# Hybrid RWKV-7 / attention step: projections fed with x times coefficient, final norm by rows, x updated from PSUM

## What is computed

```python
def rmsnorm(x, g):
    return x * rsqrt(mean(x * x, -1) + RMS_EPS) * g
def modulate(h, shift, scale):
    return h * (1 + scale) + shift
...
for l in range(2):
    if l == 1:                                   # shared_kv
        h = modulate(rmsnorm(x, kv_norm_g), shift, scale)
        k, v = split(h @ w_kv + b_kv);  k = rope_partial(k, pos)
    h = modulate(rmsnorm(x, norm_g[l, 0]), sh1, sc1)
    y = time_mix(h) if l == 0 else window_attn(h @ at_w_q + at_b_q, k, v) @ at_w_o + at_b_o
    x = x + g1 * y
    h = modulate(rmsnorm(x, norm_g[l, 1]), sh2, sc2)
    x = x + g2 * hier_moe(h)                     # top 2 of 32 experts, silu(gate) * up, down
return rmsnorm(x, final_norm_g)
```

## Time and profile before

| | before |
|---|---|
| runs (us) | 1261.39, 1262.22, 1257.76; median 1261.39 |
| profiled execution: time, span | 1259.24, 1257.0 |
| busy: PE, DVE, ACT, POOL | 1103.0, 577.8, 339.5, 32.0 |
| mean granted clock of PE | 0.938 of full |
| bytes moved, mean rate | 304.95 MB, 243 GB/s |

### The profile page before, as it was taken

One profiled execution on the slowest core, in us unless ns is written; L12 is line 12 of the kernel. 1 busy time (PEld: TensorE's weight loads), 2 busy tenths in 40 slices (PEclk: granted clock), 3 DMA queues, 4 the chain that ended last, 5 costly groups with the idle time before them and its releaser, 6 DMA issues.

```text
span 1257.0 us, 23844 instructions
## 1 busy us (share of the span) xinstructions
PE 1103.0 (88%) x9637; PEld 646.9 (51%) x9637; DVE 577.8 (46%) x1446; ACT 339.5 (27%) x651; POOL 32.0 (3%) x50
## 2 busy tenths in 40 slices
PE   6699999999988884999999977987886799999983
PEld 3355555787887453344444435666654344444442
DVE  3802165654522536355555454243146355555554
ACT  1231140122213013333333222235213333333222
POOL 0200000000000002000000000000002000000000
PEclk9799999999999797999999998987897899999996
DMA  9868755665232553899999990052053599999951
GB/s 338 191 234 299 270 212 190 203 222 200 98 137 55 192 201 126 292 394 394 394 394 394 394 391 33 13 183 86 1 198 128 222 394 394 394 394 394 394 218 43
DMA packets 114934, 304.95 MB, mean 243 GB/s; under 512 B 7268, under 2 KB 8904, under 8 KB 107688
## 3 DMA queue, kind: packets, MB, share of 16 engines
q1 hardware_dynamic: 110544, 289.78, 62.5%
q0 software_dynamic: 4112, 13.97, 4.0%
q10 hardware_dynamic: 200, 0.06, 0.0%
HBM read 298.93 MB, written 4.86 MB: 242 GB/s over the span
## 4 chain that ended last, share of the span: by engine, by line
PE 59%; SPq 21%; DVE 8%; DMA 5%; issue 3%; ACT 3%; POOL 1%; ACTq 0%; DVEq 0%; POOLq 0%
PE bank L719 57%; SPq L533 15%; SPq L538 5%; DVE work L1538 2%; DMA ring<-in_moe_w_gu 2%; DMA ring<-in_ada_w 2%; ACT work L1289 2%; DVE work L1544 1%; DVE work L1541 1%; DMA work<-h_rows,work 1%; DVE rstd L1576 1%; POOL work L659 1%; DVE att L1985 1%; ACT ring L1289 0%; PE bank L1245 0%
## 5 line engine op out<-in xcount | busy, mean ns | idle before, releaser
L719 PE MATMUL bank<-ring,work 128*64 128x512 f32 (+1 forms) x1760 | 353.2, 553 | 24.8 <-DMA ring<-in_moe_w_gu 11.7
L719 PE MATMUL bank<-work,ring 128*128 128x320 f32 (+4 forms) x1648 | 305.1, 366 | 17.4 <-DVE work L1541 7.0
L719 PEld LDWEIGHTS bank<-work,ring 128*128 128x128 f32 (+3 forms) x1648 | 211.4, 168 | 121.5 <-issue 39.8
L719 PEld LDWEIGHTS bank<-ring,work 128*64 128x64 f32 (+1 forms) x1760 | 119.0, 138 | 234.4 <-issue 230.6
L719 PE MATMUL bank<-work 128*128 128x320 bf16 (+11 forms) x1732 | 198.9, 281 | 22.5 <-DVE work L1538 7.8
L719 PEld LDWEIGHTS bank<-work 128*128 128x128 bf16 (+2 forms) x1732 | 148.1, 122 | 89.4 <-issue 26.0
L1289 ACT ACTIVATE work<-bank 128x512 f32<-128x512 f32 (+5 forms) x111 | 53.8, 517 | 209.9 <-PE bank L719 155.1
L1901 DVE TENSOR_TENSOR work<-work,bank 128x320 f32<-128x320 f32 x256 | 107.4, 481 | 1.3 <-PE bank L719 1.3
L719 PEld LDWEIGHTS bank<-ring 64*64 64x64 f32 (+2 forms) x2624 | 89.3, 136 | 20.3 <-issue 12.6
L719 PE MATMUL bank<-ring 64*64 64x64 f32 (+2 forms) x2624 | 96.5, 225 | 3.1 <-issue 2.1
L1889 DVE TENSOR_REDUCE small<-bank 64x1 f32<-64x3 f32 x64 | 10.1, 158 | 166.6 <-PE bank L719 165.6
(11 more groups left out here) (190 smaller groups left out, 794.0 us busy)
## 6 DMA issues: line engine op xcount, KB each, us to landing
ring<-in_moe_w_gu SPq DMA_DIRECT2D x128, 1024.0 KB, 14.9
ring<-in_moe_w_down SPq DMA_DIRECT2D x64, 1024.0 KB, 13.9
ring<-in_ada_w SPq DMA_DIRECT2D x35, 1024.0 KB, 5.1
ring<-in_rw_w_rkv SPq DMA_DIRECT2D x6, 2048.0 KB, 7.8
ring<-in_ada_w SPq DMA_DIRECT2D x4, 2048.0 KB, 17.9
ring<-in_kv_ada_w SPq DMA_DIRECT2D x8, 1024.0 KB, 4.8
work<-in_ada_w SPq DMA_DIRECT2D x5, 1024.0 KB, 6.2
ring<-in_rw_w_o SPq DMA_DIRECT2D x2, 2048.0 KB, 11.7
```

Of the source, the lines that this page charges most:

```text
L719: return eng.matmul(out, l, r, start=start, stop=stop, **kw)
```

## The change

- **Projections fed early.** `hkv` and `haq` become x times `coef` (norm gain times 1 + scale), without the norm factor and without the shift. ACT makes `hkv` a chunk at a time as soon as that chunk of x is final, then `haq`. The shifts are two further columns (one for each sequence): 322 columns instead of 320. PE projects outputs 0 and 1 of `kv`, then does the sum of squares, then outputs 2 and 3. The squares are DVE's.
- **Factor at eviction.** DVE multiplies each output by the factor and adds the bias to the two shift columns (`scaled`); ACT adds those as the bias, for each sequence (`biased`). So an output is evicted by 4 instructions on 2 engines in place of 1.
- **x from PSUM.** In pair 15 DVE first adds the finished `ysum` to x (`sum_to_x`), then adds the results of pairs 14 and 15 straight from PSUM to x, two instructions a chunk. Pair 0's result is copied to `ysum`, so its memset goes. `y_added` starts at 8, not 1, with all waits on it moved to match.
- **Final norm by rows.** PE transposes x itself (chunks 0 to 3 once they are final, then 4 to 7); ACT squares the token rows from PSUM and sums along them; 3 short DVE operations and a root; 6 DVE products write `ytok`, and SP writes it out in 6 DMAs of half rows. `gain_row` is loaded by POOL, 128 copies of 4 KB.
- **Filler.** PE does 5 matmuls of 512 columns ahead of the gather's transposes and 4 behind them, into a bank that nobody reads.
- In layer 0 both `coefficients` move from behind the expert loop to just ahead of `passes`.

```diff
-hkv, haq, q, qt, oT = E[1], E[5], E[6], E[7], E[5]
+gain_row = wk(D)
+row_sq = wk(6).rearrange("p (j h) -> p j h", j=3)
+row_ms = wk(3)
+TS = T + 2
+q, qt, oT = E[6], E[7], E[5]
+haq = work[:, 6 * B - C * TS:6 * B].rearrange("p (c t) -> p c t", c=C)
+hkv = work[:, 8192 - C * TS:8192].rearrange("p (c t) -> p c t", c=C)
...
+    for j, (t0, k) in enumerate(TILES):
+        for hf in range(2):
+            cols = slice(512 * hf, 512 * hf + 512)
+            sp.wait("ytok", j, hf)
+            dst = o[1][0][:, cols] if j == 2 else o[0][0, t0:t0 + k, cols]
+            eng.dma_start(dst, ytok[0:k, j, cols]).then_inc(in_sems["y_written"], 16)
...
+    eng.dma_start(gain_row, i["final_norm_g"].rearrange("(a d) -> a d", a=1).broadcast_to([P, D])
+                  ).then_inc(in_sems["gain_in"], 16)
...
+    def keep_busy(n):
+        pb = bank.spare()
+        for _ in range(n):
+            ins = mm(pb[:, :], ident, const[:, 0:512], True, True)
+        pe.did(ins)
...
+        keep_busy(5)
...
+        keep_busy(4)
         pe.wait("passes", l)
...
-        pe.wait("x begun", l)
+        while bank.n % 8:
+            bank.n += 1
+        return nb
     moe(0)
+    project("kv", range(2), hkv, lambda hf: ("wkv",), ("h", "KV"))
     mean_square("A1")
-    project("kv", range(4), hkv, lambda hf: ("wkv",), ("h", "KV"))
+    pe.wait("x moe", 0)
+    project("kv", range(2, 4), hkv, lambda hf: ("wkv",))
...
+    pe.wait("shifts")
...
-    moe(1)
-    mean_square("F")
-    pe.wait("h", "F")
-    for j, (t0, k) in enumerate(TILES):
-        for hf in range(2):
-            pb = bank.open("ytok", j, hf)
+    nb = moe(1)
+    for hf in range(2):
+        eng.wait_ge(moe_sems[1]["y_added"], 128 * nb + 4 * hf + 4)
+        for j, (t0, k) in enumerate(TILES):
+            b = 3 * hf + j
+            if b == 3:
+                pe.wait("x moe", 1)
+            pb = bank.open("xt", j, hf)
             for cc in range(4):
-                ins = eng.transpose(pb[0:k, P * cc:P * cc + P], E[1][:, 4 * hf + cc, t0:t0 + k], ident)
-            full(ins, "ytok", j, hf)
+                ins = eng.transpose(pb[0:k, P * cc:P * cc + P], x[:, 4 * hf + cc, t0:t0 + k], ident)
+            full(ins, "xt", j, hf)
...
+    nb = moe(0)
+    ac.wait("coef", "A1")
+    for c in range(C):
+        eng.wait_ge(moe_sems[0]["y_added"], 128 * nb + c + 1)
+        for r, t0, k in SEQS:
+            act(hkv[:, c, t0:t0 + k], x[:, c, t0:t0 + k], ACT.Identity, ("h", "KV", c),
+                scale=coef2[:, 0, r, c:c + 1])
+    ac.wait("x moe", 0)
+    for c in range(C):
+        for r, t0, k in SEQS:
+            act(haq[:, c, t0:t0 + k], x[:, c, t0:t0 + k], ACT.Identity, ("h", "A1", c),
+                scale=coef2[:, 1, r, c:c + 1])
     root("A1")
-    modulated("KV", E[0], hkv)
...
+    def biased(n, dst, *keys):
+        ac.wait("scaled", n)
+        for r, t0, k in SEQS:
+            act(dst[:, t0:t0 + k], dst[:, t0:t0 + k], ACT.Identity, *keys, bias=bcol[:, n, r:r + 1])
+    for c in range(2):
+        biased(c, kraw[:, c, :], ("kraw", c))
+    for c in range(2):
+        biased(2 + c, vT[:, c, :], ("vT", c))
...
-        act(q[:, c, :], pk("q", c)[:, 0:T], ACT.Identity, ("read", "q", c), ("qraw", c),
-            bias=vcol("at_b_q", c))
+        biased(4 + c, q[:, c, :], ("qraw", c))
...
-    squares("F")
-    root("F")
...
+    act(small[0:1, 14:15], cst("ident")[0:1, 0:1], ACT.Sqrt)
+    ac.wait("sums zeroed", 1)
+    for hf in range(2):
+        for j, (t0, k) in enumerate(TILES):
+            act(work[0:k, 512 * (3 * hf + j):512 * (3 * hf + j) + 512],
+                pk("xt", j, hf)[0:k, :], ACT.Square, ("row squares", j, hf),
+                accum_out=row_sq[0:k, j, hf:hf + 1])
+    ac.wait("row ms")
+    act(row_ms, row_ms, ACT.Sqrt, ("row root",))
...
-        op(eng.memset(ysum[:, :, :], 0.0))
+        op(eng.memset(row_sq, 0.0), ("sums zeroed", l))
...
         op(eng.memset(xcols[:, :, NA:XC], 0.0))
+        if l == 0:
+            ve.wait("h", "B0", C - 1)
+            coefficients("KV", vcol("kv_norm_g", 0, C))
+            coefficients("A1", vcol("norm_g", 16, C))
...
-        def added(i, u, cc):
+        def gate(r, c):
+            return mod[:, l, r, 40 + c:40 + c + 1]
+        def added(i, u, cc, where):
             for c in cc:
                 eng.wait_ge(S["y_made"], 8 * i + c + 1)
-                eng.tensor_tensor(ysum[:, c, :], ysum[:, c, :], ps[y_bank(u, c)][:, 0:T],
-                                  A_).then_inc(S["y_added"], 1)
-        def pair(i, u, e_next, first_pair):
+                y = ps[y_bank(u, c)]
+                if where == "new":
+                    ins = eng.tensor_copy(ysum[:, c, :], y[:, 0:T])
+                elif where == "sum":
+                    ins = eng.tensor_tensor(ysum[:, c, :], ysum[:, c, :], y[:, 0:T], A_)
+                else:
+                    for r, t0, k in SEQS:
+                        ins = eng.scalar_tensor_tensor(x[:, c, t0:t0 + k], y[:, t0:t0 + k], gate(r, c),
+                                                       x[:, c, t0:t0 + k], M, A_)
+                ins.then_inc(S["y_added"], 1)
+        sums = 2 if l == 0 else 1
+        def sum_to_x(p):
+            for c in range(C):
+                for r, t0, k in SEQS:
+                    ins = eng.scalar_tensor_tensor(x[:, c, t0:t0 + k], ysum[:, c, t0:t0 + k], gate(r, c),
+                                                   x[:, c, t0:t0 + k], M, A_)
+            ins.then_inc(S["x_summed"], 1)
+            if l == 0:
+                eng.wait_ge(S["x_summed"], sums * p + 1)
+                for r in range(2):
+                    ins = eng.tensor_copy(hkv[:, :, T + r], kvmod[:, r, 0:C])
+                ins.then_inc(S["x_summed"], 1)
+        def pair(i, u, e_next, where, last=None):
+            if last is not None:
+                eng.wait_ge(S["y_added"], 8 * i)
+                sum_to_x(last)
+                eng.wait_ge(S["x_summed"], sums * last + sums)
             weigh(i, u)
-            if not first_pair:
-                added(i - 1, 1 - u, range(6))
+            if where:
+                added(i - 1, 1 - u, range(6), where)
...
-            if not first_pair:
-                added(i - 1, 1 - u, range(6, C))
+            if where:
+                added(i - 1, 1 - u, range(6, C), where)
             if e_next is not None:
...
-            pair(16 * p, 0, 4, True)
-            pair(16 * p + 1, 1, 4, False)
+            pair(16 * p, 0, 4, None)
+            pair(16 * p + 1, 1, 4, "new")
             with eng.Fori(1, EXP // 4 - 1) as k_:
                 for u in range(2):
-                    pair(16 * p + 2 * k_ + u, u, 4 * k_ + 4, False)
-            for u in range(2):
-                pair(16 * p + 14 + u, u, None, False)
-            added(16 * p + 15, 1, range(C))
+                    pair(16 * p + 2 * k_ + u, u, 4 * k_ + 4, "sum")
+            pair(16 * p + 14, 0, None, "sum")
+            pair(16 * p + 15, 1, None, "x", last=p)
+            added(16 * p + 15, 1, range(C), "x")
...
-        eng.wait_ge(S["y_added"], 128 * nb + 1)
-        for c in range(C):
-            for r, t0, k in SEQS:
-                stt(x[:, c, t0:t0 + k], ysum[:, c, t0:t0 + k], mod[:, l, r, 40 + c:40 + c + 1],
-                    x[:, c, t0:t0 + k], M, A_, *([("x begun", l)] if c == r == 0 else []),
-                    ("x for", "A1" if l == 0 else "F", c // 2))
+        eng.wait_ge(S["y_added"], 128 * nb + 8)
+        op(eng.memset(small[:, 13:14], 0.0), ("x moe", l))
         ve.settle()
     moe(0)
-    coefficients("KV", vcol("kv_norm_g", 0, C))
-    coefficients("A1", vcol("norm_g", 16, C))
+    for b in range(4):
+        tt_(sq_buf("A1")[:, 2 * b:2 * b + 2, :], x[:, 2 * b:2 * b + 2, :], x[:, 2 * b:2 * b + 2, :], M,
+            ("squares", "A1", b))
+    for r in range(2):
+        op(eng.tensor_copy(haq[:, :, T + r], mod[:, 1, r, 0:C]), ("shifts",))
     rms("A1")
     ve.settle()
-    normed("KV", E[0])
-    modulated("KV", E[0], hkv, range(C - ACT_CHUNKS))
-    modulated("A1", E[0], haq, range(C))
+    def scaled(n, dst, bias, *key):
+        pb = pk(*key)
+        ts(bcol[:, n, :], pb[:, T:TS], bias, None, A_, ALU.bypass)
+        tt_(dst, pb[:, 0:T], rstd[:, :], M, ("read",) + key, ("scaled", n))
+    for c in range(4):
+        scaled(c, kraw[:, c, :] if c < 2 else vT[:, c - 2, :], vcol("b_kv", c), "kv", c)
...
+    def rotated(c):
...
+    for c in range(C):
+        scaled(4 + c, q[:, c, :], vcol("at_b_q", c), "q", c)
+        if c:
+            rotated(c - 1)
+    rotated(C - 1)
...
-    rms("F")
+    eng.wait_ge(in_sems["gain_in"], 16)
+    for j in range(3):
+        ve.wait("row squares", j, 1)
+    op(eng.tensor_reduce(row_ms, row_sq, AX.X, A_))
     ve.settle()
-    normed("F", E[0])
-    for c in range(C):
-        ts(E[1][:, c, :], E[0][:, c, :], vcol("final_norm_g", c), None, M, ALU.bypass, ("h", "F"))
+    ts(row_ms, row_ms, 1.0 / D, RMS_EPS, M, A_, ("row ms",))
+    ve.wait("row root")
```

(7 more changed lines are left out.)

66 lines of the change are left out of this document (32 added, 34 removed).

## The result

| | before | after |
|---|---|---|
| runs beside each other (us) | 1256.63 to 1262.22, median 1259.58 | 1224.87 to 1233.28, median 1228.09 |
| profiled execution: time, span | 1259.24, 1257.0 | 1225.86, 1224.1 |
| mean granted clock of PE | 0.938 | 0.954 |

A forecast was written before the change was run, and what follows sets the result against it. Expert loops stream weights at the DMA's rate, the rest being short serial work. Terms +0.2 - 2.0 - 12.7 + 0.8 - 11.7 = -25.4 us gave 1233.8 to 1236.0, so 1235.0; range 1228 to 1243.

The forecast's parts named there:

- part 5: End of the kernel, from x whole through transposes, squares and products to the output writes: -11.7 us, bounds -9.5 and -13.
- 7.4 us of landing and closing to the span's end: Time from the last output DMA issue to the span's end in the old kernel; only 0.4 us less to land forecast.
- Part 1: Entry of the expert loops, with coefficients moved ahead and filler for PE's clock: +0.2 us in layer 0, -2.0 in layer 1.
- 0.9 of 1.8 in layer 0: Entry of layer 0's expert loop: filler gives back 0.9 of the 1.8 us lost at 1.2 GHz.
- Part 2: Last pair of each expert loop: sum_to_x hidden with 0.7 us to spare, adds ahead of the hidT copy cost PE +1.15 us.
- rival B: Last pair of each loop: sum_to_x isn't hidden, up to 5 us a layer; 1241 us for 3 a layer; 6%.
- Part 3: From layer 0's final scatter to the end of the KV projection: -12.7 us, bounds -10.5 and -14.
- over 0.27: Length in us of a 322-column matmul record above which such matmuls would count as slowed.
- rival D: Projections: 96 matmuls of 322 columns run slower than those of 320; 1288 us at twice as long; 3%.
- Rival C: KV projection, layer 0: ACT can start hkv only when x is whole, PE idles and loses its clock; 1241 us; 5%.
- Part 4: Queries: 322 columns instead of 320 and a longer eviction of the last output; +0.8 us, bounds +0.3 and +1.6.
- Rival A: Clock falls at the seams: filler gives nothing back, KV projection, final transposes and half-row writes are slow; 1242 us; 11%.

The follow-up runs named there:

- a_no_filler: The changed kernel without its filler matmuls (five in the wait for the gather, four behind its transposes) in both layers; median 1227.94 us, ratio 0.9758 to the kernel before.
- a_factor_first: The changed kernel with the KV projection held back until the norm factor is there, the sum of squares first; median 1233.32 us, ratio 0.9812 to the kernel before.
- a_pool_out: The changed kernel with its six half-row output transfers issued by POOL instead of SP; median 1230.38 us, against 1225.26 for the unaltered changed kernel.
- b_sp_out: The kernel before with its three whole-row output transfers issued by SP instead of POOL; median 1253.77 us against 1257.93, ratio 0.9966.
- a_whole_rows: The changed kernel with three whole-row output transfers by SP instead of six of half rows; median 1230.28 us, ratio 0.9778 to the kernel before.

## Why the prediction was off

The step that failed is a term of part 5, the "7.4 us of landing and closing to the span's end", which the forecast carried over less 0.4. It measured 2.2 behind the last issue's end where 6.87 stood, and 0.45 less outside the span: 4.75 of the 6.4 us by which the forecast was short. The paths of parts 2, 3 and 5 were right.

**Part 1, entries.** Layer 1: -2.0 forecast, -2.1 measured over four profiles, but as a mean of two cases (-2.6 when the clock held, three of four, and -0.7 when not), not as the partial recovery that I took: that the numbers meet is luck. Layer 0: the coefficients cost 1.1 us as priced (pause 3.31 against 2.21). The 0.9 us that filler was to give back did not come: nine of nine first products behind 3.31 us lost the clock. Measured +1.2 against +0.2. The smaller step that failed here is "0.9 of 1.8 in layer 0": I scaled the recovery with the length of the pause, and the products took either 7.09 us or 8.41 and more; behind one and the same pause of 1.97 us they took 7.09 or 8.78. The rule that I weighed: the Trainium skill ("TensorE: Matmul & The Clock Gate", Part 4: PE-mode transpose) says that transposes don't count as activity of PE, by which the filler would have started at 1.2 GHz. Its four products took 3.60 us directly behind the transposes in both layers, near what I had worked out for full clock (3.45), so the trace again speaks against the rule. `a_no_filler` does so more plainly: PE did nothing but transposes from 487.01 to 495.1, and its granted clock was 0.50 from 489 to 491, 0.81 in the next 2 us and 1.00 in the 2 behind.

**Part 2.** 0.81 us of idling left where 0.7 was forecast, the scatter 1.05 later (1.15). Right; rival B is out.

**Part 3.** 26.6 us from scatter to the end of the KV outputs, forecast 26.7; the sum of squares stands in their middle. Right, and `a_factor_first` shows the cause. 322-column records take 8.85 / 32 = 0.277 us, which is 4.3 us an output, as with 320 columns: the "over 0.27" that I named as the sign of rival D was set too tight, D is out all the same. Rival C is out: there is no pause ahead of the projection.

**Part 4.** From the scatter to ranking 1 -14.35 against -13.05. Up to the keys' turn it is as forecast (and 1.4 less in the one of four where the scatter took 3.71 us). From there to ranking 1 it took 170.1 to 170.9 us where 170.7 stood, so the +0.8 did not come. The 322 columns cost their share (33.63 us from the first query product to the last output's first, 33.38 before); the 0.5 for the last output's eviction is not to be seen, as from there to the output projection it took 69.9 to 70.7 us, 70.8 before. What makes this last stretch vary by 0.7 us I didn't trace.

**Part 5, the end.** Two terms were mis-sized. The first is the closing named above, by far the largest error of the whole: it was carried over as if it belonged to any last transfer. I saw in the diff that SP writes in place of POOL and priced the pieces, not the queue. `a_pool_out` (+5.1) and `b_sp_out` (-4.2) show it. The 0.4 for the halved last transfer had no row behind it; `a_whole_rows` has 0.6. The second: the last product ends 8.1 us after x is whole (1213.2 to 1221.33), not 9.4, mostly because the squares end at 1216.3, 3.1 behind x, where I had 4.0: the second half of the transposes begins 0.64 behind x (I had 0.9) and runs at full clock, and a square takes 0.58 (I had 0.7).

**Rival A** happened in part: the clock fell at layer 0's entry, sometimes at layer 1's, and in the scatters (5.11 instead of 3.71). But it didn't fall behind the scatter of layer 0, where the chain has no pause any more.

**The range.** With the closing term right the forecast would have been 1230.3 (1235.0 - 4.7) in a range of 1223 to 1238, with 1226.8 to 1228.1 well inside. The range had no case in which the closing itself shrinks, although no row bounded it: for an operation that changes its issuer, "stays" was one end of a range and not its middle.

## What to carry to other kernels

Look at who issues the very last transfers: here the choice of engine was worth 4 to 5 us, a seventh of the whole gain, for one moved loop. A norm factor that scales whole columns can be applied at eviction, and the gain (9 us here) is that of the products which then run in the shade of the factor's chain. Filler for the clock has to be long enough: with pauses of 3.3 and 2.2 us left it never kept the clock here, with 2.0 in five of eleven, with 0.7 and less always; nothing between 0.74 and 1.97 was run.
